# Later modulation vectors in steps of 1,024 columns, reduced by 32x32 transposes on VectorE, and the first two vectors with the ada matrix as the stationary operand

## The chip, the cores and the metric

The kernel runs on 1 core of one Trainium2 chip. The metric is device time in microseconds of that core, from its start to its end, as the median of several runs; lower is better. All arithmetic is fp32 or sums of fp32r products (each operand split into a high part and a remainder, three products kept).

## The reference, cut to what matters

Two transformer blocks run one after the other on a sequence of 512 tokens of width 1024. Each block takes six modulation vectors (shift, scale and gate, once for the mixer and once for the feed-forward part) from a small condition vector. The first block also needs the first two of them for a context of 256 tokens, from a second condition vector.

```python
def adaln(cond, w, b):
    return jnp.split(jax.nn.silu(cond) @ w + b, N_MOD, axis=-1)      # w: 1024 x 6144

# first block
sh_a, sc_a, gt_a, sh_f, sc_f, gt_f = adaln(c, w_ada[0], b_ada[0])
csh_a, csc_a, ...                  = adaln(c_ctx, w_ada[0], b_ada[0])
h_ctx = modulate(rms_norm(ctx, g_mix_pre), csh_a, csc_a)
h_lat = modulate(rms_norm(x, g_mix_pre), sh_a, sc_a)
x = x + gt_a * rms_norm(token_mixer(h_lat, ...), g_mix_post)
x = x + gt_f * rms_norm(conv_ffn(modulate(rms_norm(x, g_ffn_pre), sh_f, sc_f), ...), g_ffn_post)
# second block: the same six vectors from silu(c_2) @ ada_w_2 + ada_b_2, a hybrid mixer, a SwiGLU
```

The products of a condition vector with its matrix (w_ada, ada_w_2) are the subject here: 12 vectors of 1024 values, so 48 MB of weights that are each used once.

## The kernel before, in words

Activations lie with the features on the 128 partitions and the 512 tokens along the free dimension (8 tiles of 128x512). Weights stream from HBM in 110 chunks of 128x2048 (1 MB) through two buffers `raw`; ScalarE makes the high part WH of a chunk (`split_hi`), VectorE the remainder WL (`split_lo`), and TensorE multiplies both with the high and low parts of the activations: three fp32r matmuls for every product (`mm3`, L1158 to L1162). The order of all work is written out by hand: each engine has its own program (`@block.sync`, `.scalar`, `.vector`, `.tensor`), and counting semaphores tie them. The stages in order are: start (norm statistics and the first two modulation vectors), k and v, q, retention, Fourier mix, gate, output projection (C_OUT), the up projection with a convolution (C_UP, 22 tiles, a hardware loop `Fori` of 11 passes on every engine), the down projection (C_DOWN, 12 chunks), then the second block (C_U, C_K2, C_V2, C_Q2, C_GATES, attention, C_MERGE, C_O, C_UP2, C_DOWN2).

The modulation vectors are made in two ways.

The first two (shift and scale of the first mixer, for the tokens and for the context) are made at the start. Eight chunks `adaf` of 128x2048 (256 columns of the matrix for all 1024 rows) are loaded first of all. For each chunk TensorE holds the two condition vectors as the stationary operand (128x2, `csil`) and streams 256 columns of the matrix past them, 8 times with accumulation (L1227). The result is two rows of 256 values; ScalarE copies four pieces of 512 of them out of PSUM (L405, `m0row`), and TensorE turns them into columns with a 2x2 identity (`mod0_turn`, L1220). Between chunks TensorE also sums squares for the norms of the context (L1232) and of x (L1235). VectorE then adds the bias (L769) and the norms and the first projection follow. A matmul of fp32 operands shows in the trace as two passes, each with a weight load of its own.

The other ten vectors are made during the later stages, in 40 jobs of 256 columns (`ada_job`, L715). A job loads 128x2048 in two halves `ada_half`, and VectorE multiplies each of 8 pieces of 128x256 by one column of the condition vector and adds it to `ada_acc` (L706, L708). The remaining sum over the 128 partitions is TensorE's (`ada_sum`, L1192 to L1195): two fp32 matmuls with 128 columns of `ada_acc` as the stationary operand and a column of ones as the moving one. These calls stand between the projections in TensorE's program: after every k/v, q, f, g and out chunk, once in each pass of the up loop, after every one of the 12 down chunks and after the 4 chunks of C_U. VectorE adds the bias in `modulation` (L993) before a vector is needed.

VectorE's program puts a job behind a `split_lo` or behind the last use of a tile; in the last part of a stage the output tiles (`out_tile`, L941) come behind it.

Of the kernel before, what the change touches and what calls it, by code (L numbers as in the profile page):

```python
# [19 lines left out]
P = 128  # L20
# [30 lines left out]
ADA_LATER = 40  # L51
JOBS_UP = 14
JOBS_DOWN = JOBS_UP + FT // 2

# [25 lines left out]
def build(nc, weights, ada, x_t, ctx_t, vecs, rope, band, pos, csd, masks, out):  # L80
# [4 lines left out]
    with stack:  # L85
# [17 lines left out]
        csil_up = fix("csil_up", [P, FT // 2, KT])  # L103
        rstd = fix("rstd", [P, L])
        scratch = fix("scratch", [P, 2, L])
        ada_acc = fix("ada_acc", [P, 2, 256])
        mod0 = fix("mod0", [P, 16, 2])
        mod = fix("mod", [P, 2 * ADA_LATER])
# [4 lines left out]
        ident2 = fix("ident2", [2, 2])  # L113
# [7 lines left out]
        ada_half = fix("ada_half", [P, 2, CH // 2])  # L121
# [13 lines left out]
        m0row = over("m0row", [2, 16 * P], U + 64 * KB)  # L135
# [33 lines left out]
        spL = (over("spL0", [P, 1280], H0 + 5 * KB, R), over("spL1", [P, 1280], U + 101 * KB, R))  # L169
# [4 lines left out]
        mask_in = over("mask_in", [P, 4, P], U + 58 * KB)  # L174
        lnsq = over("lnsq", [P, CT, L], U + 96 * KB)
        cH, cL = over("cH", [P, CT, L], U, R), over("cL", [P, CT, L], U + 8 * KB, R)
        assert U + 106 * KB <= nc.sbuf_usable_end, (U, nc.sbuf_usable_end)
# [66 lines left out]
        def _(sp):  # L244
            sp.dma_start(vec[:, :], vecs).then_inc(s.vec_in, 16)
            sp.dma_start(ctxT[:, :, :], ctx_t).then_inc(s.ctx_in, 16)
            sp.dma_start(ident2[:, :], masks[0:2, 0, 0:2]).then_inc(s.ident2_in, 16)
# [9 lines left out]
            for j in range(2):  # L257
                sp.dma_start(ada_half[:, j, :], ada[ADA_FIRST, :, j * (CH // 2):(j + 1) * (CH // 2)])\
                    .then_inc(ada_in[j], 16)
# [8 lines left out]
            def load_half_job(a, j):  # L268
                sp.wait_ge(s.ada_read, 2 * a + (j - 1))
                sp.dma_start(ada_half[:, j, :], ada[a + ADA_FIRST, :, j * (CH // 2):(j + 1) * (CH // 2)])\  # L270
                    .then_inc(ada_in[j], 16)

            def load_job(a):

                for j in range(2):
                    load_half_job(a, j)

            job = 1  # L280
            for c in range(2, C_UP + 3):
                load_chunk(c, c % 2)
                if c == 2 or c - 2 in (C_DFT + 1, C_G):
                    continue
                load_job(job)
                job += 1
            assert job == JOBS_UP + 1, job
            load_chunk(C_UP + 3, 1)

            with sp.Fori(0, FT // 2) as i:  # L290
                for j in range(2):
                    load_chunk(2 * i + (C_UP + 4 + j), j)
                    load_half_job(i + JOBS_UP + 1, j)

            load_job(JOBS_DOWN + 1)
            with sp.Fori(0, 6) as i:
                for j in range(2):
                    load_chunk(2 * i + (C_DOWN + 4 + j), j)
                    load_job(2 * i + (JOBS_DOWN + 2 + j))
            load_chunk(C_DOWN + 16, 0)  # L300
            load_job(ADA_LATER - 1)
            load_chunk(C_DOWN + 17, 1)
# [32 lines left out]
        def _(act):  # L335
# [67 lines left out]
            for q in range(4):  # L403
                act.wait_ge(s.mod0_sum, 2 * q + 2)
                A(m0row[:, 4 * P * q:4 * P * (q + 1)], bank[q][0:2, :], ACT.Copy).then_inc(s.mod0_row, 1)  # L405
                if q == 2:

                    act.wait_ge(s.csd_in, 16)
                    A(csdH[:, :], csd_in[:, :], ACT.Copy).then_inc(s.csd_hi, 1)
                    split_hi(0, 0, True)  # L410
# [172 lines left out]
            with act.Fori(0, FT // 2) as i:  # L583
                for j in range(2):
                    for x, tmp in enumerate((tA, tB)):
                        act.wait_ge(s.mm_done, 32 * i + done(C_UP + j, x, 2))

                        w = VAT["cw"] + 2 * FT + x * FT + j
                        b = VAT["cb"] + x * FT + j
                        A(tmp[:, j, :], bank[2 * j + x][:, :], ACT.Identity, bias=vec[:, bass.ds(2 * i + b, 1)],  # L590
                          scale=vec[:, bass.ds(2 * i + w, 1)]).then_inc(s.conv_mid, 1)
                    split_hi(2 * i + (C_UP + j + 2), j)
                    act.wait_ge(s.bank_free, 4 * i + (B_UP + 2 * j + 1))
                    A(tA[:, j, :], tA[:, j, :], ACT.Silu).then_inc(s.ffn_silu, 1)
                    act.wait_ge(s.ffn_mul, 2 * i + j + 1)
                    A(GH[:, bass.ds(2 * i + j, 1), :], tB[:, j:j + 1, :], ACT.Copy).then_inc(s.ffn_hi, 1)
# [94 lines left out]
        def _(dve):  # L691
# [8 lines left out]
            def ada_half_job(a, slot, half, c_col):  # L700

                dve.wait_ge(ada_in[half], 16 * a + 16)
                for k in range(4):
                    w = ada_half[:, half, 256 * k:256 * k + 256]
                    if half == k == 0:
                        ins = TS(ada_acc[:, slot, :], w, c_col(0), None, mult)  # L706
                    else:
                        ins = STT(ada_acc[:, slot, :], w, c_col(4 * half + k), ada_acc[:, slot, :], mult, add)  # L708
                    if k < 3:
                        own.link(ins)  # L710
                    else:
                        ins.then_inc(s.ada_read, 1)
                        dve.wait_ge(s.ada_read, 2 * a + (half + 1))

            def ada_job(a, slot, c_col, first=False):  # L715
                if not first:
                    dve.wait_ge(s.ada_summed, a - 1)
                for half in range(2):
                    ada_half_job(a, slot, half, c_col)

            ada_next = [0]

            def ada_now():
                a = ada_next[0]
                ada_next[0] += 1
                ada_job(a, a % 2, (lambda k: csil[:, k, 0:1]) if a < 16 else (lambda k: csil2[:, k:k + 1]), a < 2)
# [31 lines left out]
            for i in range(FT // 2):  # L758
                own.link(V.tensor_copy(csil_up[:, i, :], csil[:, :, 0] if JOBS_UP + i < 16 else csil2[:, :]))
# [6 lines left out]
            dve.wait_ge(s.mod0_done, 4)  # L766
# [30 lines left out]
            for p in range(2):  # L797
# [18 lines left out]
                ada_now()  # L816
# [9 lines left out]
                ada_now()  # L826
# [8 lines left out]
            for p in range(2):  # L835
# [7 lines left out]
                if p == 0:  # L843
                    states_lo(1)
                    ada_now()
# [46 lines left out]
            ada_now()  # L892

            for p in range(2):
# [7 lines left out]
                if p == 0:  # L902
                    ada_now()
            for g in range(GROUPS + 1):
# [9 lines left out]
                if g in (1, 2):  # L914

                    a = ada_next[0]
                    if g == 1:
                        dve.wait_ge(s.ada_summed, a - 1)
                    ada_half_job(a, a % 2, g - 1, lambda k: csil[:, k, 0:1])
                    ada_next[0] += g - 1  # L920
# [30 lines left out]
            def add_and_norm(m, free0):  # L951
# [3 lines left out]
                if m == 0:  # L955
                    modulation(13, 8, 24, 2)
# [13 lines left out]
            def out_phase(m, c0, free0, jobs=0):  # L970
                post_gain(m)
                for p in range(4):
                    split_lo(c0 + p + 1, (p + 1) % 2)
                    for _ in range(jobs):
                        ada_now()
# [4 lines left out]
            def down_phase(m, c0, free0, skip):  # L980
                post_gain(m)
                for p in range(4):
                    for j in range(3):
# [3 lines left out]
                        if m == 1:  # L987
                            ada_job(a, (a + 1) % 2, lambda k: csil2[:, k:k + 1])
# [716 lines left out]
```

## Time and profile before

| | |
|---|---|
| time, median of 3 runs | 1509.86 us (1508.96 to 1511.58) |
| the profiled execution's own time | 1509.9 us |
| its span | 1508.1 us |
| granted TensorE clock, mean over the span | 0.972 |
| TensorE busy with matmuls | 1435.9 us, 95%, 6532 instructions |
| VectorE busy | 913.5 us, 61% |
| ScalarE busy | 521.4 us, 35% |
| DMA | 173.56 MB, mean 115 GB/s |

TensorE's busy time is made of instructions that overlap each other, so the useful figure is the pace: the distance from one start to the next. A clock of 1.00 in a row is the upper of two levels (2.4 GHz), 0.50 the lower (1.2 GHz). The record of the clock begins at 14.7 us; the rows before that show 1.00, and there only the pace of the matmuls tells the level. A wait in brackets at the end of a row is idle time of that engine before it and what ended it.

### The profile page before, as it was taken

To read this page: it belongs to the slowest core of one execution; us is meant where nothing else is said; L and a number is where in the kernel's file an instruction comes from. 1 tells how busy PE (TensorE), PEld (TensorE's weight loads), DVE (VectorE), ACT (ScalarE), POOL (GpSimd) and SP (SyncE) were. 2 spreads that over 40 slices of the span, in tenths; PEclk is the share of its full clock that TensorE was granted. 3 is DMA by queue.
4 is the path that set the end of the run, shared out by engine and by line. 5 is a ranking of instruction groups with operands and counts; after the bars stand their busy time and mean duration, and the time that the engine had idled before them with its cause. 6 is when DMAs were issued, how large, how long until landed. Compare 5 with 4: busy or idle time off the path is not lost.

```text
span 1508.1 us, 17436 instructions
## 1 busy us (share of the span) xinstructions
PE 1435.9 (95%) x6532; PEld 1150.3 (76%) x6532; DVE 913.5 (61%) x1263; ACT 521.4 (35%) x661; POOL 26.4 (2%) x22
## 2 busy tenths in 40 slices
PE   7899999979999999998899999999979999999995
PEld 3698588848888888886689887668848888888884
DVE  2776864877677677676669883766564333332334
ACT  4432433334343433222421223773233232323211
POOL 0000000010000000001000000000010000000001
PEclk9999999979999999999899999899989999999998
DMA  9234033613434435564232222002302322222321
GB/s 394 96 116 151 13 126 136 213 56 114 164 125 147 145 126 191 193 214 168 71 132 96 101 86 82 1 1 84 112 28 84 111 84 103 92 93 102 112 84 56
DMA packets 31018, 173.56 MB, mean 115 GB/s; under 512 B 3445, under 2 KB 3701, under 8 KB 15477
## 3 DMA queue, kind: packets, MB, share of 16 engines
q1 hardware_dynamic: 30964, 172.83, 31.9%
q8 instruction: 36, 0.59, 0.2%
q14 instruction: 18, 0.14, 0.0%
HBM read 170.72 MB, written 2.10 MB: 115 GB/s over the span
## 4 chain that ended last, share of the span: by engine, by line
PE 91%; DVE 5%; ACT 2%; issue 1%; DMA 0%; SPq 0%; DVEq 0%; ACTq 0%
PE bank L1160 27%; PE bank L1161 27%; PE bank L1162 27%; PE bank L1227 2%; PE bank L1413 2%; PE bank L1573 1%; DVE xT L959 1%; DVE tmp L734 1%; PE bank L1335 1%; DVE yT L958 1%; PE bank L1559 1%; PE bank L1195 1%; PE bank L1560 1%; PE bank L1548 0%; DVE ada_acc L708 0%
## 5 line engine op out<-in xcount | busy, mean ns | idle before, releaser
L1160 PE MATMUL bank<-hH,WH 128*128 128x512 f32 x1088 | 431.3, 396 | 16.9 <-DVE hL L739 16.9
L1161 PE MATMUL bank<-hL,WH 128*128 128x512 f32 x1088 | 426.8, 392 | 0.0
L1162 PE MATMUL bank<-hH,WL 128*128 128x512 f32 x1088 | 426.7, 392 | 0.0
L698 DVE TENSOR_TENSOR WL<-raw,WH 128x2048 fp32r<-128x2048 f32 x110 | 252.0, 2291 | 165.7 <-ACT WH L343 165.0
L343 ACT ACTIVATE WH<-raw 128x2048 fp32r<-128x2048 f32 x110 | 210.1, 1910 | 150.5 <-PE bank L1162 149.7
L1160 PEld LDWEIGHTS bank<-hH,WH 128*128 128x128 f32 x1088 | 206.7, 190 | 62.6 <-issue 20.3
L1161 PEld LDWEIGHTS bank<-hL,WH 128*128 128x128 f32 x1088 | 206.8, 190 | 43.1 <-issue 1.0
L1162 PEld LDWEIGHTS bank<-hH,WL 128*128 128x128 f32 x1088 | 206.4, 190 | 43.5
L1160 PE MATMUL bank<-GH,WH 128*128 128x512 f32 x352 | 137.9, 392 | 0.0
L1161 PE MATMUL bank<-GL,WH 128*128 128x512 f32 x352 | 136.9, 389 | 0.0
L1162 PE MATMUL bank<-GH,WL 128*128 128x512 f32 x352 | 136.9, 389 | 0.0
L708 DVE SCALAR_TENSOR_TENSOR ada_acc<-ada_half,csil,ada_acc 128x256 f32<-128x256 f32 x203 | 98.4, 485 | 7.4
L1147 DVE TENSOR_TENSOR tB<-tA,bank 128x512 f32<-128x512 f32 x22 | 15.1, 688 | 113.0 <-PE bank L1162 113.0
L1063 DVE SCALAR_TENSOR_TENSOR cacc<-uT,vec,cacc 128x511 f32<-128x511 f32 (+29 forms) x120 | 78.6, 731 | 0.0
L1162 PEld LDWEIGHTS bank<-GH,WL 128*128 128x128 f32 x352 | 66.1, 188 | 13.8
L1160 PEld LDWEIGHTS bank<-GH,WH 128*128 128x128 f32 x352 | 66.1, 188 | 13.3
L1161 PEld LDWEIGHTS bank<-GL,WH 128*128 128x128 f32 x352 | 66.1, 188 | 13.2
L944 DVE TENSOR_SCALAR yT<-bank,gp 128x512 f32<-128x512 f32 x32 | 23.9, 751 | 47.8 <-ACT scratch L541 44.5
L541 ACT ACTIVATE scratch<-bank 128x512 f32<-128x512 f32 x28 | 16.8, 600 | 101.5 <-PE bank L1162 101.3
L684 ACT ACTIVATE tA<-bank 128x512 f32<-128x512 f32 x22 | 13.2, 599 | 94.7 <-PE bank L1162 94.7
L708 DVE SCALAR_TENSOR_TENSOR ada_acc<-ada_half,csil_up,ada_acc 128x256 f32<-128x256 f32 x77 | 37.2, 484 | 9.6
L1227 PE MATMUL bank<-adaf,csil 128*2 128x256 f32 x128 | 31.2, 405 | 9.0 <-DMA adaf<-ada 9.0
(255 smaller groups left out, 1872.5 us busy)
## 6 DMA issues: line engine op xcount, KB each, us to landing
raw<-weights SPq DMA_DIRECT2D x110, 1024.0 KB, 4.7
ada_half<-ada SPq DMA_DIRECT2D x80, 512.0 KB, 3.8
adaf<-ada SPq DMA_DIRECT2D x8, 1024.0 KB, 17.6
xT<-x_t SPq DMA_DIRECT2D x2, 1024.0 KB, 11.8
out_t<-xT SPq DMA_DIRECT2D x8, 256.0 KB, 2.0
ctxT<-ctx_t SPq DMA_DIRECT2D x1, 1024.0 KB, 5.1
ropeT<-rope SPq DMA_DIRECT2D x1, 512.0 KB, 21.8
bandT<-band SPq DMA_DIRECT2D x1, 448.0 KB, 19.5
```

What stands on the lines that cost most here:

```text
L343: A(WH[:, slot, :], raw[:, slot, :], ACT.Copy).then_inc(s.hi_done, 1)
L541: A(to, bank[n % 4][:, :], ACT.Square).then_inc(s.ysq_ready, 1)
L698: TT_(WL[:, slot, :], raw[:, slot, :], WH[:, slot, :], sub).then_inc(s.lo_done, 1)
L708: ins = STT(ada_acc[:, slot, :], w, c_col(4 * half + k), ada_acc[:, slot, :], mult, add)
L944: TS(yT[:, n, :], bank[n % 4][:, :], gp[:, n:n + 1], None, mult).then_inc(s.bank_free, 1)
L1063: STT(cacc[:, k, shift:L], uT[:, k, 0:L - shift], w, cacc[:, k, shift:L], mult, add)\
L1147: TT_(tB[:, j, :], tA[:, j, :], bank[2 * j + 1][:, :], mult).then_inc(s.bank_free, 2)
L1160: mm(o, lh, rh, start=start, stop=False, skip_group_check=skip)
L1161: mm(o, lh, rl, start=False, stop=False, skip_group_check=skip)
L1162: return mm(o, ll, rh, start=False, stop=stop, skip_group_check=skip)
L1227: ins = mm(bank[c // 2][0:2, 256 * (c % 2):256 * (c % 2) + 256], csil[:, k, :], adaf[:, c, 256 * k:256 * k + 256], start=(k == 0), stop=(k ...
L1413: mm(bank[5][:, :], ones[:, :], squares[k % 4], start=(k == 0), stop=(k == KT - 1))\
```

## The change

The first two vectors: for each chunk, 128 columns of the matrix are now the stationary operand and the two condition vectors (128x2) the moving one, so the result stands in columns at once. The copies by ScalarE (`m0row`), the turns by TensorE and the small identity go.

The later vectors: a step is now one row block of 128 rows times 1,024 columns; 8 steps make one whole vector (a group), 80 steps all ten. Each step is one VectorE instruction on 128x1024. After the eighth VectorE transposes the accumulator in blocks of 32x32 (into the weight buffer) and sums along the free axis, which leaves, for each quarter of the partitions, the partial sums of 32 columns in `quarter`. TensorE adds the four quarters with a stacked identity `selT`, for one, two or four vectors at a time (`mod_sum`), in 5 places in all. The loops of the up stage of the first block are written out on all four engines. Some buffers are placed elsewhere (`lnsq`, `spL`, `mask_in`), and the loads of the steps replace those of the half jobs in the sync queue, two for one.

```diff
-                for k in range(KT):
-                    ins = mm(bank[c // 2][0:2, 256 * (c % 2):256 * (c % 2) + 256], csil[:, k, :],
-                             adaf[:, c, 256 * k:256 * k + 256], start=(k == 0), stop=(k == KT - 1))
+                for j in range(2):
+                    t = 2 * c + j
+                    for k in range(KT):
+                        at = 256 * k + P * j
+                        ins = mm(bank[4][:, 2 * t:2 * t + 2], adaf[:, c, at:at + P], csil[:, k, :], start=(k == 0),
+                                 stop=(k == KT - 1), skip_group_check=True)
                 ins.then_inc(s.mod0_sum, 1)
...
-                if c >= 3 and c % 2:
-                    mod0_turn(c // 2 - 1)
-            mod0_turn(3)
...
-            def ada_sum(a, slot, col):
-                pe.wait_ge(s.ada_read, 2 * a + 2)
-                for j in range(2):
-                    ins = mm(bank[7][:, col(j)], ada_acc[:, slot, P * j:P * j + P], ones[:, 0:1], start=True, stop=True,
-                             skip_group_check=True)
-                ins.then_inc(s.ada_summed, 1)
+            def mod_sum(first, groups):
+                pe.wait_ge(s.ada_read, KT * (first + groups))
+                for q in range(4):
+                    at = 32 * first + q
+                    ins = mm(bank[7][32 * q:32 * q + 32, KT * first:KT * (first + groups)], selT[:, :],
+                             quarter[:, at:at + 32 * groups - 3:4], start=True, stop=True, skip_group_check=True)
+                ins.then_inc(s.mod_summed, 1)
...
+            def ada_step():
+                a = ada_next[0]
+                ada_next[0] += 1
+                group, k = divmod(a, KT)
+                w = ada_half[:, a % 2, :]
+                c_col = csil[:, k, 0:1] if group < 4 else csil2[:, k:k + 1]
+                dve.wait_ge(ada_in[a % 2], 16 * (a // 2) + 16)
+                if k == 0:
+                    TS(ada_acc[:, :], w, c_col, None, mult).then_inc(s.ada_read, 1)
+                    return
...
+                ins = STT(ada_acc[:, :], w, c_col, ada_acc[:, :], mult, add)
+                if k < KT - 1:
+                    ins.then_inc(s.ada_read, 1)
+                    return
+                own.link(ins)
+                own.link(V.transpose(w, ada_acc[:, :]))
+                V.tensor_reduce(quarter[:, 32 * group:32 * group + 32], w.rearrange("p (b i) -> p b i", i=32),
+                                mybir.AxisListType.X, add).then_inc(s.ada_read, 1)
...
-            with pe.Fori(0, FT // 2) as i:
-                for j in range(2):
-                    have(2 * i + (C_UP + j))
...
+            for t in range(FT):
+                j = t % 2
+                have(C_UP + t)
```

The five calls of `mod_sum` on TensorE stand behind the gate chunks (one vector), before the norm sum of the first output projection (two), behind the up stage (two), behind the fourth down chunk (one) and behind C_Q2 (four). VectorE takes two steps where it took a job, with these exceptions: the four parts of the first output projection take 2, 1, 1 and 0 steps; each of the 22 up tiles takes one step (before: half a job); the four chunks of C_U take 3, 3, 3 and 1.

## Rows read from the trace of the kernel before

**Rows 1.** The chain that ended last, shares of the span by engine (page).
```profile
PE 91%; DVE 5%; ACT 2%; issue 1%; DMA 0%; SPq 0%; DVEq 0%; ACTq 0%
```
**Rows 2.** The waits of TensorE: waiting line, releaser, us in total, times, longest.
```profile
PE bank L1413 <- ACT scratch L387: 18.1, 6, 5.3
...
PE bank L1160 <- DVE aF L879: 3.7, 1, 3.7
```
**Rows 3.** Timeline, TensorE in the start stage: start us, us, line, count.
```profile
9.02 6.40 PE L1227 MATMUL bank<-adaf,csil 128*2 128x256 f32 x16 [9.02 <-DMA adaf<-ada]
...
15.97 7.07 PE L1227 MATMUL bank<-adaf,csil 128*2 128x256 f32 x32
22.97 1.12 PE L1235 MATMUL bank<-sqacc,ones 128*128 128x512 f32 x2
...
43.53 1.94 PE L1220 MATMUL bank<-ident,m0row 2*128 2x2 f32 x16
```
**Rows 4.** Timeline, VectorE at the end of the start stage.
```profile
45.51 0.18 DVE L769 TENSOR_TENSOR mod<-bank,vec 128x16 f32<-128x16 f32 x1 [4.83 <-PE bank L1220]
```
**Rows 5.** Timeline, TensorE in attention, lower clock, 128-column loads.
```profile
952.73 0.41 PE L1559 MATMUL bank<-spH,maskR 128*128 128x128 f32 x1
952.94 0.41 PE L1560 MATMUL bank<-spL,maskR 128*128 128x128 f32 x1
953.15 0.52 PE L1559 MATMUL bank<-spH,maskR 128*128 128x256 f32 x1
```
**Rows 6.** Line L1560, its weight loads: ns min/median/max, first and last start.
```profile
L1560 PEld LDWEIGHTS bank<-spL,maskR x80: 187/192/333, 942.5 to 1013.5; 128*128 128x128 f32 x80
```
**Rows 7.** Windows: us, busy us (count) of PE, PEld, DVE, ACT, POOL, clock, DMA.
```profile
48.00:50.00 2.00, 0.91 (x2) 0.83 (x3) 2.00 (x4) 1.40 (x3) 0.00 (x0) 0.70 0.00 0
52.00:54.00 2.00, 2.00 (x9) 1.59 (x9) 2.00 (x4) 1.11 (x2) 0.00 (x0) 0.94 0.00 0
332.00:334.00 2.00, 0.37 (x1) 0.40 (x2) 2.00 (x4) 1.58 (x3) 0.00 (x0) 0.53 0.00 0
338.00:340.00 2.00, 2.00 (x8) 1.61 (x7) 2.00 (x4) 1.24 (x2) 0.00 (x0) 0.76 0.00 0
```
**Rows 8.** Windows in attention, the same columns.
```profile
940.00:942.00 2.00, 2.00 (x10) 1.20 (x9) 0.81 (x3) 1.86 (x7) 0.00 (x0) 1.00 0.00 0
942.00:944.00 2.00, 2.00 (x12) 1.62 (x12) 1.15 (x4) 1.94 (x5) 0.00 (x0) 0.78 0.00 0
```
**Rows 9.** Line L1195, the sums over partitions.
```profile
L1195 PE MATMUL bank<-ones,ada_acc x160: 164/250/250, 87.1 to 777.2; 128*128 128x1 f32 x160
```
**Rows 10.** Timeline, TensorE around one such sum in the up stage.
```profile
347.09 0.50 PE L1195 MATMUL bank<-ones,ada_acc 128*128 128x1 f32 x4
347.45 0.48 PE L1160 MATMUL bank<-hH,WH 128*128 128x512 f32 x1
347.77 0.39 PE L1161 MATMUL bank<-hL,WH 128*128 128x512 f32 x1
348.00 0.39 PE L1162 MATMUL bank<-hH,WL 128*128 128x512 f32 x1
```
**Rows 11.** Groups of VectorE by form: count, busy us, mean ns, idle us before.
```profile
L708 DVE SCALAR_TENSOR_TENSOR ada_acc<-ada_half,csil,ada_acc 128x256 f32<-128x256 f32 x203 | 98.4, 485 | 7.4
...
L1063 DVE SCALAR_TENSOR_TENSOR cacc<-uT,vec,cacc 128x510 f32<-128x510 f32 x4 | 2.8, 747 | 0.0
```
**Rows 12.** Timeline, VectorE in the q stage.
```profile
141.92 3.61 DVE L708 SCALAR_TENSOR_TENSOR ada_acc<-ada_half,csil,ada_acc 128x256 f32<-128x256 f32 x7
...
152.87 0.69 DVE L786 TENSOR_TENSOR qtmp<-bank,ropeT 128x512 f32<-128x512 f32 x1
```
**Rows 13.** Timeline, ScalarE in the q stage.
```profile
151.08 0.59 ACT L422 ACTIVATE qtmp<-bank 64x512 f32<-64x512 f32 x1
```
**Rows 14.** Timeline, VectorE at the end of the down stage.
```profile
705.12 0.75 DVE L944 TENSOR_SCALAR yT<-bank,gp 128x512 f32<-128x512 f32 x1
```
**Rows 15.** Timeline, TensorE at the end of the down stage.
```profile
706.52 1.13 PE L1406 MATMUL bank<-sqacc,ones 128*128 128x512 f32 x2 [0.80 <-DVE sqacc L949]
```

More of the change, by code:

```diff
@@ L300, in _, with load_step @@
-            load_chunk(C_DOWN + 16, 0)
-            load_job(ADA_LATER - 1)
-            load_chunk(C_DOWN + 17, 1)
+            def load_step(a):
+                sp.wait_ge(s.ada_read, a - 1)
+                sp.dma_start(ada_half[:, a % 2, :], ada_later[a]).then_inc(ada_in[a % 2], 16)
+            for c in range(2, C_OUT):
+                load_chunk(c, c % 2)
+                if c == C_G + 1:
+                    load_step(16)
+                    load_step(17)
+                elif c not in (2, C_G):
+                    load_step(2 * c - 4)
+                    load_step(2 * c - 3)
@@ L304, in _ @@
+            for q in range(12):
+                load_step(STEPS_DOWN + 2 + 2 * q)
+                load_step(STEPS_DOWN + 3 + 2 * q)
+                load_chunk(C_DOWN + 4 + q, q % 2)
+            for i in range(4):
+                for a in range(STEPS_U + 2 + 3 * i, min(STEPS_U + 5 + 3 * i, STEPS)):
+                    load_step(a)
+                if i < 2:
+                    load_chunk(C_U + 4 + i, i % 2)
             sp.wait_ge(s.mm_done, 16 * C_U)
@@ L715, in ada_job @@
[L715 to L719, printed above, removed]
             ada_next = [0]
-            def ada_now():
+            def ada_step():
                 a = ada_next[0]
                 ada_next[0] += 1
-                ada_job(a, a % 2, (lambda k: csil[:, k, 0:1]) if a < 16 else (lambda k: csil2[:, k:k + 1]), a < 2)
+                group, k = divmod(a, KT)
[5 more added lines that the diff above has]
+                    return
+                if k == 1 and group:
+                    dve.wait_ge(s.ada_read, a)
+                elif k > 1 or group:
+                    dve.wait_ge(s.ada_read, a)
+                else:
+                    dve.wait_ge(s.ada_read, 1)
+                ins = STT(ada_acc[:, :], w, c_col, ada_acc[:, :], mult, add)
[6 more added lines that the diff above has]
+                                mybir.AxisListType.X, add).then_inc(s.ada_read, 1)
@@ L728, in norm_lo, with ada_steps @@
+            def ada_steps(n):
+                for _ in range(n):
+                    ada_step()
             def norm_lo(m, tmp, src, width, hi, lo, shift, gain, mul_s, hi_s, lo_s, root=rstd):
@@ L973, in out_phase @@
                     split_lo(c0 + p + 1, (p + 1) % 2)
-                    for _ in range(jobs):
-                        ada_now()
+                    ada_steps(steps[p])
                     out_tile(m, 2 * p)
@@ L1035, in _ @@
+            modulation(3, 24, 32)
+            modulation(3, 32, 40)
             down_phase(1, C_DOWN, B_DOWN, 0)
@@ L1083, in _ @@
                 conv_taps(11)
+                if p == 1:
+                    modulation(5, 48, 80)
                 if p == 6:
@@ L1432, in out_phase @@
                         project_pair(0, src_h, src_l, order, ready, 2)
-                    for _ in range(jobs if p < 3 else 0):
-                        ada_now()
+                if m == 0:
+                    mod_sum(1, 2)
                 out_stat(m)
-                for _ in range(jobs):
-                    ada_now()
                 if m < 3:
@@ L1508, in _ @@
                     ins.then_inc(s.mm_done, step(n, 2))
+            mod_sum(6, 4)
             for i in range(16):
```

278 lines of the change are left out of this document (105 added, 173 removed).

## The prediction

> **What bounds the kernel now.** I read the chain that ended last first: TensorE holds 91% of it, VectorE 5% [rows 1]. So an edit on VectorE counts only where TensorE waits for it, and every instruction taken from TensorE's stream counts almost anywhere. The waits say where that is not so: TensorE waits mostly at the four norms (18.1 us for ScalarE's squares), which the change leaves alone, and once for 3.7 us behind VectorE between q and retention [rows 2]. Then I read the timeline of the start, because there the change alters TensorE's own work. TensorE begins at 9.02 us, when the first chunk has landed, and from then on is never idle: the first 16 passes take 6.40 us (0.40 us each), the next 32 take 7.07 us (0.22 us each), so it starts at the lower clock and reaches the upper one around 15 us; the turns end the stage and VectorE goes on at 45.51 us [rows 3, 4]. The stage is TensorE's from 9.02 to 45.5 us.
>
> **Part 1, the start: from 128 passes to 256.** Before, 8 chunks x 8 row blocks x 2 passes = 128 passes, each with a 2-column load and 256 streamed columns. After, 8 x 2 x 8 = 128 matmuls, 256 passes, each with a 128-column load and 2 streamed columns. The 32 turns go. What counts now is the pace of a 128-column load.
>
> At the upper clock the nearest row is the last set of turns: 16 passes with 128-column loads and 2 streamed columns in 1.94 us, 0.12 us each [rows 3]. At the lower clock I have no row with so few streamed columns; the nearest are the pairs in attention with 128-column loads and 128 streamed columns, which follow each other at 0.21 us (952.73, 952.94, 953.15) [rows 5]; the load itself lasts 333 ns there and 187 to 192 ns at the upper clock [rows 6]. Bounds for a pass at the lower clock: not under 0.12 us, the pace at the upper clock, and not over 0.33 us, the load if nothing overlaps it. I take 0.213 us, since the row is of the same load.
>
> Which clock? The stage begins at the lower one. Before, a dense stream lifted it. Now two columns are streamed per pass. The row that decides for me is in attention: from 940 to 944 us TensorE is busy without a gap (10 and 12 instructions in 2 us), with a load ahead of each matmul, and yet the clock falls inside the second window (mean 0.78) [rows 8]. These are matmuls of 64 rows with 128 to 512 columns, far more streaming than two columns. So loads one behind the other do not hold the clock up, and I expect them not to lift it: the whole stage runs at 1.2 GHz.
>
> The sum: 256 x 0.213 = 54.5 us. The two norm sums between the chunks run at the lower clock too: two passes of 256 columns at 0.40 us = 0.8 us, and the 512-column one twice its 1.06 us (22.97 to the next start) = 2.1 us [rows 3]. The end is 9.02 + 54.5 + 2.9 = 66.4 us, VectorE goes on at 66.6 instead of 45.5: **+21.1 us**. Nothing hides it: the norm and the first projection need these vectors. The removed copies of ScalarE and the 11 small copies of VectorE lay beside TensorE's work: 0.
>
> After the stage TensorE idles some 3.5 us and starts the first projection at the lower clock in both kernels. Before, that lasted from 49.1 to about 52.2 us (means 0.70 and 0.94); at another restart from about 333.6 to 338.9 us (0.53 and 0.76) [rows 7]. Half of such a stretch is lost, so the difference lies between -1 and +1.5 us: **+0.5**.
>
> The Trainium skill says otherwise on the load. Its page "TensorE: Matmul & The Clock Gate", section "LDWEIGHTS (loading the stationary operand)", prices a load at its columns over 1.2 GHz, so 107 ns at either clock. The trace disagrees: 192 against 333 ns [rows 6]. By the page an estimate of the 256 passes is 27 us and the start would end before 40 us.
>
> **Part 2, the sums on TensorE.** Before, 160 passes at L1195 [rows 9], 40 calls of 4. Around one: start 347.09, next projection matmul 347.45, the one after 347.77, then the usual 0.23 [rows 10]. So 0.36 us for the four, and the first matmul behind them takes 0.32 instead of 0.23: 0.45 us a call. Of the 40, five lie where TensorE waits anyway: two in the q stage ahead of the 3.7 us wait [rows 2], one ahead of the wait for the gate's silu, one behind the norm sum of the first output projection, and the last of the down stage (part 4). 35 x 0.45 = **-15.75 us**.
>
> Added are 5 calls of 4 matmuls, 8 passes, with 32-column loads and 8 to 32 columns streamed. No row has them; at the pace of L1195 (0.09 us each, and 0.09 behind them) a call costs 0.8 us, as an upper bound; the lower is 0.2 us. I take 0.8. The first stands ahead of the silu wait and is hidden; four count, also the one ahead of L1406, where TensorE came straight from the projection: **+3.2 us**.
>
> **Part 3, VectorE.** A multiply-add of 256 columns takes 485 ns, one of 510 columns 747 ns [rows 11]: 1.03 ns a column, so 1,024 columns cost 0.485 + 768 x 0.00103 = 1.28 us. A job was 8 instructions, 4.0 us; two steps are 2.6 us. Ten times come a transpose and a reduction of 1,024 columns, not in the trace: between half and twice the pace of the multiply-add, so 0.5 to 2.1 us each; I take 1.1. In the last step of a group VectorE then has 2.2 us more, so 4.8 instead of 4.0 us for a pair: hidden, because in the long stages a projection pair lasts 10.9 us (48 x 0.227 us) and VectorE needs 7 to 10 us of it. Without that cover each would cost up to 4.2 us. The later `modulation` calls wait for sums that TensorE has passed already; the one for the last 32 columns moves behind 11 convolution taps and nothing waits for it. In sync's queue every load of a step stands behind a wait that is met before the chunk load that follows it; only a third step in C_U finds its data late by some 2 us, within the slack of 10.9.
>
> In the q stage VectorE is what TensorE waits for: the seven multiply-adds from 141.92 last 3.61 us, then WL, and the last rope tile starts at 152.87 [rows 12]. Two steps are 1.4 us shorter; ScalarE's swap for that tile ends at 151.67 [rows 13], 1.2 us earlier, and moves up with the 0.45 us of the removed sum, so it is no bound: **-1.4 us**.
>
> **Part 4, the end of the down stage.** VectorE reaches the last two output tiles at 705.12 [rows 14], behind a job; TensorE has been done with its projection since 705.2 and starts L1406 at 706.52, after a wait of 0.80 us [rows 15]. With two steps VectorE is 1.4 us earlier, L1406 starts at 705.3, and the last square of ScalarE is ready when it ends: **-1.2 us**, the removed sum included.
>
> **Loops written out.** Inside the loop the pace is 0.23 us as elsewhere, no gap at a turn: 0. Written-out stages elsewhere run at the same pace, so fetching more code costs nothing I can see; bounds -0.2 and +2 us.
>
> **The sum** against the profiled span: 1508.1 + 21.1 + 0.5 - 15.75 + 3.2 - 1.4 - 1.2 = 1514.6 us. The execution's own time is 1.8 us above its span (1509.9) and within 0.1 us of the median, so **1516.3 us**: slower by 0.4%, because 15 us gained in later stages are overpaid by 21.6 us at the start.
>
> **Rivals.** *The clock rises during the start (faster).* If loads with two streamed columns count as work, or if their pace does not hang on the clock, the passes run at 0.12 us after the first 6.4 us (30 passes): 9.02 + 6.4 + 226 x 0.12 + 1.6 = 44.1 us, 1.4 us earlier than before instead of 21.1 later, and no other term changes: 1516.3 - 22.5 = 1493.8 us. For it: before, the clock rose within 7 us of steady work [rows 3]. Against: it fell in attention under unbroken pairs [rows 8]. It decides where the stage ends before about 57 us (1516.3 - 9.5 = 1506.8); a rise at 30 us would do, with 95 passes before it and 161 behind: an end near 50 us and 1500 us in all. The same page of the Trainium skill, in "What's actually happening", says that activity releases the throttle and speaks of whatever is issued, which by itself would be this rival; the trace bears the first half out, the second not. Chance 0.11.
>
> *Nothing overlaps the load.* 256 x 0.333 = 85 us, 30.7 more: 1547 us. For it only the 333 ns; against it, 0.21 us between two such loads [rows 5]. Chance 0.04.
>
> *VectorE comes late.* Transposes at 2.1 us and late third steps push it over the 10.9 us of a pair in the up stage or C_U; three or four stalls of 1 to 2 us: 1521 us. Chance 0.05.
>
> **How the numbers follow.** The forecast has 0.80; its own range is 1509 to 1524 us (pace 0.20 to 0.24 us: -3 and +7; sums 5 us cheaper to 1 dearer). That range with the third rival holds 0.8, so the range is 1508 to 1524. What a measurement of this kernel can tell from no change is about 0.2%, 1506.8 to 1512.9 us. Faster 0.14 (first rival, and a tail of the forecast), same 0.09, slower 0.77.
>
> **What would show it.** Right: L1227's successor with 256 passes at about 0.21 us, VectorE's first mod0 addition near 66.6 us, 40 passes of `mod_sum` in place of 160, no gap of TensorE behind the last down chunk, and from the first projection on about 15 us less than before. Wrong: a pace near 0.12 us in the start or a clock record that begins there at 1.00; a new wait of TensorE for VectorE in the up stage or the convolution; a gain in the later stages under 10 us, which would mean that the 0.45 us are not saved.

## The result and the profile after

The changed kernel takes **1518.85 us** (median of 4 runs, 1518.31 to 1521.63), the one before on the same chip 1509.49 us (4 runs, 1508.96 to 1511.58): ratio 1.0063, 95% interval 1.0046 to 1.0081. 1516.3 us had been forecast. The profiled execution took 1518.31 us, its span is 1516.4 us, 8.3 us more than before.

The page of the changed kernel: span, busy time by engine, shares of the chain that ended last, and three groups (count, busy us, mean ns, idle us before).
```profile
span 1516.4 us, 16108 instructions
...
PE 1444.9 (95%) x6508; PEld 1176.0 (78%) x6508; DVE 880.0 (58%) x1033; ACT 516.2 (34%) x657; POOL 26.4 (2%) x22
...
PE 90%; DVE 6%; ACT 2%; issue 1%; DMA 1%; SPq 0%; DVEq 0%; ACTq 0%
...
L1196 PE MATMUL bank<-csil,adaf 128*128 128x2 f32 x256 | 54.7, 352 | 8.9 <-DMA adaf<-ada 8.9
L1196 PEld LDWEIGHTS bank<-csil,adaf 128*128 128x128 f32 x256 | 55.2, 333 | 10.1 <-issue 9.9
L713 DVE SCALAR_TENSOR_TENSOR ada_acc<-ada_half,csil,ada_acc 128x1024 f32<-128x1024 f32 x70 | 89.7, 1281 | 11.4 <-DMA ada_half<-ada_later 9.1
```
The chain has the same shape as before [rows 1]: TensorE still sets the time, so the 8.3 us must be in its own stream. L1196 has 256 loads with a mean of 333 ns, the figure that the loads of the lower clock have in [rows 6]. That is the first term of the prediction in one row.

The start stage of the changed kernel, TensorE's timeline; it answers to [rows 3].
```profile
8.93 6.96 PE L1196 MATMUL bank<-csil,adaf 128*128 128x2 f32 x32 [8.93 <-DMA adaf<-ada]
15.75 1.20 PE L1201 MATMUL bank<-csqacc,ones 128*128 128x256 f32 x2
16.74 13.65 PE L1196 MATMUL bank<-csil,adaf 128*128 128x2 f32 x64
30.25 2.05 PE L1204 MATMUL bank<-sqacc,ones 128*128 128x512 f32 x2
32.10 34.13 PE L1196 MATMUL bank<-csil,adaf 128*128 128x2 f32 x160
69.86 0.77 PE L1148 MATMUL bank<-hH,WH 128*128 128x512 f32 x1 [3.62 <-DVE hL L738]
```
The same stage on VectorE; it answers to [rows 4].
```profile
66.27 0.17 DVE L766 TENSOR_TENSOR mod<-bank,vec 128x16 f32<-128x16 f32 x1 [27.22 <-PE bank L1196]
```
160 passes in 34.13 us are 0.213 us each, from the first to the last. VectorE goes on at 66.27 us, where 66.6 was forecast.

Windows of the changed kernel in this stage: us, busy us (count) of PE, PEld, DVE, ACT, POOL, granted clock, DMA share, GB/s.
```profile
20.00:66.00 46.00, 46.00 (x211) 44.97 (x211) 5.82 (x10) 7.78 (x19) 0.00 (x0) 1.00 0.52 215
```
Here is a trap. The clock column says 1.00 while the loads last 333 ns. It says 1.00 at the start of the kernel before too, where 16 passes of 256 columns take 6.40 us [rows 3]. The column has no record until the clock changes for the first time, and nothing changed it here: the record of the changed kernel begins at 73.5 us, where the 512-column matmuls of the first projection go from 0.43 us to 0.23 us each. The duration of a known load is the safer reading: 192 ns at 2.4 GHz, 333 ns at 1.2 GHz.

Next I followed the distance between the same matmul in both traces (after minus before). It is +20.8 us at the first projection, +22.3 in the k/v stage, +16.2 ahead of the first norm behind it (309 us in the kernel before), +6.7 just before attention, +10.2 behind it, and +8.3 at the end. Two of the steps up were not in the sum. In the k/v stage TensorE waits for `ktmp` in both kernels, 2.29 us before and 2.09 us after, but only in the changed one does the clock fall behind the wait. The first row is of the kernel before, the other two of the changed one:
```profile
70.00:72.00 2.00, 2.00 (x19) 2.00 (x19) 1.07 (x2) 1.48 (x3) 0.00 (x0) 1.00 0.91 385
90.00:92.00 2.00, 1.46 (x7) 1.49 (x8) 1.09 (x2) 1.53 (x3) 0.00 (x0) 0.64 0.88 365
92.00:94.00 2.00, 2.00 (x11) 2.00 (x11) 1.58 (x3) 0.28 (x1) 0.00 (x0) 0.50 0.27 111
```
And in attention the clock falls in both kernels, for longer in the changed one. The kernel before in windows of 7 us:
```profile
943.00:950.00 7.00, 4.62 (x18) 3.65 (x17) 5.34 (x11) 4.85 (x13) 0.00 (x0) 0.51 0.00 0
950.00:957.00 7.00, 7.00 (x22) 5.11 (x21) 3.99 (x11) 5.00 (x12) 0.00 (x0) 0.52 0.02 5
957.00:964.00 7.00, 7.00 (x36) 4.78 (x37) 5.24 (x12) 4.95 (x14) 0.00 (x0) 1.00 0.00 0
```
The changed kernel, the same stage:
```profile
951.00:957.00 6.00, 3.22 (x11) 2.66 (x11) 5.12 (x10) 3.87 (x12) 0.00 (x0) 0.50 0.00 0
957.00:964.00 7.00, 7.00 (x22) 5.07 (x21) 3.79 (x11) 4.90 (x11) 0.00 (x0) 0.50 0.00 0
964.00:971.00 7.00, 7.00 (x18) 3.94 (x17) 3.40 (x8) 2.55 (x8) 0.00 (x0) 0.50 0.00 0
```
The lower clock lasts 13.7 us before (943.1 to 956.8) and 20.5 us after (950.7 to 971.2), and the distance grows by 3.45 us there. The change touches nothing in that stage but the place of the buffer `spL`. Whether it caused this was one question for the experiments.

### The profile page after: what moved, and what is told of

Same layout as the page of the kernel before. It is cut to its first block, busy times and chain, and to the rows that moved or that the text cites. A ratio compares the mean times of both kernels' runs of the same rounds, so it can differ in the third digit from the quotient of the medians.

```text
span 1516.4 us, 16108 instructions
## 1 busy us (share of the span) xinstructions
PE 1444.9 (95%) x6508; PEld 1176.0 (78%) x6508; DVE 880.0 (58%) x1033; ACT 516.2 (34%) x657; POOL 26.4 (2%) x22
## 4 chain that ended last, share of the span: by engine, by line
PE 90%; DVE 6%; ACT 2%; issue 1%; DMA 1%; SPq 0%; DVEq 0%; ACTq 0%
PE bank L1148 27%; PE bank L1150 26%; PE bank L1149 26%; PE bank L1196 4%; PE bank L1376 2%; PE bank L1528 1%; DVE xT L951 1%; DVE tmp L733 1%; PE bank L1298 1%; DVE yT L950 1%; PE bank L1514 1%; PE bank L1515 1%; DVE ada_acc L713 1%; PE bank L1503 0%; DMA adaf<-ada 0%
## 5 line engine op out<-in xcount | busy, mean ns | idle before, releaser
L713 DVE SCALAR_TENSOR_TENSOR ada_acc<-ada_half,csil,ada_acc 128x1024 f32<-128x1024 f32 x70 | 89.7, 1281 | 11.4 <-DMA ada_half<-ada_later 9.1
L1150 PEld LDWEIGHTS bank<-GH,WL 128*128 128x128 f32 x352 | 66.1, 188 | 13.7
L1196 PE MATMUL bank<-csil,adaf 128*128 128x2 f32 x256 | 54.7, 352 | 8.9 <-DMA adaf<-ada 8.9
L1196 PEld LDWEIGHTS bank<-csil,adaf 128*128 128x128 f32 x256 | 55.2, 333 | 10.1 <-issue 9.9
L1009 DVE SCALAR_TENSOR_TENSOR tB<-bank,vec,tB 128x504 f32<-128x504 f32 x22 | 16.3, 743 | 68.6 <-ACT tB L584 68.5
```

What stands on the lines that cost most here:

```text
L713: ins = STT(ada_acc[:, :], w, c_col, ada_acc[:, :], mult, add)
L1009: own.link(STT(to[:, :, 1:ROW], b[:, :, 0:ROW - 1], v("cw", w), to[:, :, 1:ROW], mult, add))
L1150: return mm(o, ll, rh, start=False, stop=stop, skip_group_check=skip)
L1196: ins = mm(bank[4][:, 2 * t:2 * t + 2], adaf[:, c, at:at + P], csil[:, k, :], start=(k == 0), stop=(k == KT - 1), skip_group_check=True)
```

## The experiments

My theory: the start costs 21 us because a pass is priced by its load, and the load's pace by the clock, which two streamed columns do not lift; the 40 small sums gave back 0.45 us each. The rivals: the pace has another cause (the chunks' DMA, the load itself), or the later part costs something that the start hides. Each kernel is compared with the kernel before on its own chip; the median of that one was 1510.4 to 1510.8 us.

**One part undone, and one part alone.** `e1_old_start` is the changed kernel with the start of before, `e2_new_start_alone` the kernel before with the new start.
```diff
 # e1_old_start, against after
-    for j in range(2):
-        t = 2 * c + j
-        for k in range(KT):
-            at = 256 * k + P * j
-            ins = mm(bank[4][:, 2 * t:2 * t + 2], adaf[:, c, at:at + P], csil[:, k, :], ...)
+    for k in range(KT):
+        ins = mm(bank[c // 2][0:2, 256 * (c % 2):256 * (c % 2) + 256], csil[:, k, :],
+                 adaf[:, c, 256 * k:256 * k + 256], ...)
+    if c >= 3 and c % 2:
+        mod0_turn(c // 2 - 1)
...
```


> The changed kernel with only its start undone: the condition vectors are stationary again, the ada chunk streams, and the copies and turns are back; the later steps, mod_sum and the written-out loops stay. Theory (slow weight loads at the lower clock cost about 21 us in the start, the rest of the change gains about 13 us net in this execution's clock phases): 1518.9 - 20.9 = 1498 us, between 1493 and 1502, first mod0 addition of VectorE back at 45.5 us. Rival (the later part gains nothing or costs by itself, and the start costs little): 1509 us or more.

> The kernel before with only the new start (ada chunk stationary, two columns streamed). Theory: 1509.5 + 21 = 1530.5 us, 256 passes at 0.213 us, first mod0 addition near 66 us. Rival (the start's cost comes from something that the later part brings with it, such as moved buffers): 1510 to 1516 us.

`e1_old_start`: 1497.94 us (6 runs, 1492.62 to 1500.74), ratio 0.9919 [0.9903, 0.9934]. `e2_new_start_alone`: 1530.55 us (4 runs), ratio 1.0137 [1.0123, 1.0152]; VectorE goes on at 66.29 us; the distance to before is +20.8 us at the first projection, +22.1 in the k/v stage and +20.9 at the end. +20.15 and -12.46 us add up to +7.7, where the medians of both parts together differ by +9.4 and their spans by +8.3. That fits within the spread of `e1_old_start`, 8 us from its fastest run to its slowest, so nothing shows that one part changes the other. The later part alone is a gain.

**Is it the clock?** `e3_warm_new_start` puts 22 matmuls of `ones` with itself ahead of the first chunk, `e4_warm_old_start` does the same to `e1_old_start`. Their results are not used.
```diff
+for _ in range(22):
+    mm(bank[7][:, 0:P], ones[:, :], ones[:, :], start=True, stop=True, skip_group_check=True)
```


> The changed kernel with 22 matmuls of ones by ones (128 columns) on TensorE before the first chunk lands, so that the clock is at its upper level when the narrow passes begin. Theory (narrow passes neither lift nor hold the clock): the first passes run at 0.11 to 0.12 us, then the clock falls and the rest at 0.213; 3 to 7 us at the upper level save as much again, 1512 to 1516 us. Rival (narrow passes can't lift the clock but hold it): all 256 at 0.12 us, 1518.9 - 22 = 1497 us. Second rival (the load pace does not hang on the clock): no change at all, 1519 us.

> e1_old_start with the same 22 matmuls of ones ahead. Theory: the first chunk's 16 passes take 3.5 instead of 6.4 us, the stage ends 2 to 3 us earlier, 1495 to 1496 us if e1 is 1498. Rival (the stage waits for the chunks' landing then): no gain over e1.

`e3_warm_new_start`: 1517.35 us (4 runs), ratio 1.0044 [1.003, 1.0059]. TensorE's timeline:
```profile
1.03 7.27 PE L1189 MATMUL bank<-ones 128*128 128x128 f32 x44 [1.03 <-POOL ones L323]
...
8.75 3.75 PE L1198 MATMUL bank<-csil,adaf 128*128 128x2 f32 x32 [0.45 <-DMA adaf<-ada]
...
13.35 13.65 PE L1198 MATMUL bank<-csil,adaf 128*128 128x2 f32 x64
```
Its windows:
```profile
8.00:12.00 4.00, 3.55 (x33) 3.39 (x31) 2.12 (x5) 1.60 (x4) 0.00 (x0) 1.00 1.02 430
12.00:14.00 2.00, 2.00 (x11) 1.82 (x10) 0.00 (x0) 0.00 (x0) 0.00 (x0) 0.57 0.99 418
14.00:20.00 6.00, 6.00 (x29) 6.00 (x30) 1.28 (x2) 2.30 (x4) 0.00 (x0) 0.50 1.02 426
```
The loads of the first chunk in this run:
```profile
L1198 PEld LDWEIGHTS bank<-csil,adaf 128*128 128x128 f32 x30 | 3.4, 192 | 0.6 <-issue 0.6
```
At the upper clock the same instruction runs at 0.113 us (32 passes start to start in 3.61 us), with the DMA as busy as elsewhere in the stage, so the pace is the clock's doing. But the narrow passes do not hold it: it falls at 12.27 us and the other 224 passes run at 0.213 again. VectorE goes on at 62.88 us, 3.4 us earlier. In the profiled execution 3.3 us of that are lost in attention: the lower clock lasts 30.7 us there, the distance to before grows by 6.8 us instead of 3.45, and the span is 1516.5 us against 1516.4.

These rows also say what makes the new start dear. An estimate from them and [rows 3]: at the upper clock the old form would cost 128 x 0.221 = 28.3 us and the new one 256 x 0.113 = 28.9 us; at the lower clock 128 x 0.40 = 51.2 and 256 x 0.213 = 54.5 us. At the same clock the two forms are nearly equal. The difference of 21 us is mostly that the stream of the old form was followed by a rise of the clock 5.7 us after it began, and the stream of the new one ran for 57 us without one.

The Trainium skill's "TensorE: Matmul & The Clock Gate", section "LDWEIGHTS (loading the stationary operand)", gives a load as its columns over 1.2 GHz, 107 ns for 128 columns, with no word on the gated clock. The pace of 113 ns at the upper clock is near that figure, the 213 ns at the lower clock is twice it; here the measurement decides.

`e4_warm_old_start` missed what I wrote: 1499.35 us (5 runs, 1497.67 to 1500.35), no better than without the 22 matmuls. Its timeline says why:
```profile
9.04 3.61 PE L1214 MATMUL bank<-adaf,csil 128*2 128x256 f32 x16 [1.15 <-DMA adaf<-ada]
...
18.76 3.62 PE L1214 MATMUL bank<-adaf,csil 128*2 128x256 f32 x16 [1.93 <-DMA adaf<-ada]
...
23.00 1.13 PE L1222 MATMUL bank<-sqacc,ones 128*128 128x512 f32 x2 [0.63 <-DVE sqacc L759]
```
The first 16 passes need 3.61 instead of 6.40 us, and then TensorE waits 1.93 us for the third chunk and 0.63 us for the squares, and is back at its old time, 23.00 against 22.97 [rows 3]. Up to there the old start has to wait for its data once TensorE is faster; the new one is paced by its loads. From 23 us on TensorE is busy without a gap in the old form too.

**Can denser work between the narrow passes hold the clock?** `e8_dense_every_second` puts one such dense matmul behind every second narrow matmul but the last of a block, `e9_dense_every_one` behind every one but the last, both on top of the 22.
```diff
 for k in range(KT):
     ins = mm(bank[4][:, 2 * t:2 * t + 2], adaf[:, c, at:at + P], csil[:, k, :], ...)
+    if k % 2 == 1 and k < KT - 1:      # e9: k % 1 == 0
+        mm(bank[7][:, 0:P], ones[:, :], ones[:, :], start=True, stop=True, skip_group_check=True)
```


> e3_warm_new_start plus one dense matmul (ones by ones, 128 columns, two passes, result unused) behind every second narrow matmul of the start, 48 in all. If this much dense work holds the clock: 256 x 0.113 + 96 x 0.107 = 39 us, the stage ends near 50 us, 16 us less than the changed kernel. If not (dense passes are then a quarter of the time): the clock falls as in e3 and the added passes cost 96 x 0.21 = 20 us, end near 83 us. I expect the second.

> The same with a dense matmul behind seven of eight narrow ones, 112 in all. If the clock holds: 256 x 0.113 + 224 x 0.107 = 53 us, end near 64 us. If not: 54.5 + 47.7 = 102 us, end near 112 us. I expect the first: a narrow pass is slow only for the clock, and at the upper level its pace is 0.113 us throughout.

`e8_dense_every_second`: 1540.59 us in one run, the clock falls at 10.72 us, VectorE goes on at 85.13. `e9_dense_every_one`: 1564.94 us in one run, it falls at 11.17, VectorE goes on at 112.0. The windows of `e9_dense_every_one`:
```profile
9.00:12.00 3.00, 3.00 (x24) 3.00 (x25) 1.33 (x4) 0.83 (x2) 0.00 (x0) 0.86 1.01 429
12.00:15.00 3.00, 3.00 (x16) 3.00 (x16) 0.00 (x0) 0.00 (x0) 0.00 (x0) 0.50 0.99 421
```
I had expected that a nearly even mix would hold the clock; it did not, though a stream of such dense matmuls alone had lifted it just before. So filling of this kind does not repair the start. The 96 passes of `e8_dense_every_second` cost 85.13 - 62.88 = 22.3 us, 0.23 us each, which is 0.21 at the lower clock and a part from the earlier fall of the clock, by 1.6 us. Wider filling, of 512 columns, was not tried here.

**The lower clock in attention.** `e1_again` is `e1_old_start` run a second time. `e5_attention_fill` adds three unused matmuls of 512 columns in each of the first five turns of attention to `e1_old_start`; `e10_before_attention_fill` adds the same to the kernel before.
```diff
+if 0 <= i <= 4:
+    for _ in range(3):
+        mm(bank[4][:, :], maskR[:, 3, :], maskR[:, :, :], start=True, stop=True, skip_group_check=True)
```


> e1_old_start once more on the same chip as e5 and e6, for its spread: median 1498 us, runs from 1492 to 1501 by the length of the lower-clock stretch in attention.

> e1_old_start plus 15 matmuls of 512 columns on masks (three in each of TensorE's first five turns of the attention loop, results unused), where TensorE waits and the clock falls. Theory A (the spread of 1491 to 1499 us of e1, and part of what the changed kernel lost against the sum, is the stretch at the lower clock in attention, 13.7, 20.5 or 30.7 us long, 0.5 us lost per us): the clock stays up, e1's profiled span less 8 to 10 us plus 2 us for the added work, 1489 to 1492 us median and a spread under 3 us. Rival B (the attention stage is slower for moved buffers): no gain, 1498 to 1500 us.

> The kernel before with the 15 filling matmuls in attention alone. Theory (the stretch at the lower clock in attention was there before too, 13.7 us in its profile, 7 us lost): the time falls by 7 - 2 = 5 us, 1505.5 us, with no lower clock in attention. Rival (only the changed later part loses its clock there): no gain, or 2 us more.

`e1_again`: 1497.56 us (4 runs, 1495.18 to 1500.3). The same kernel, profiled twice, has a span of 1491.5 and of 1498.5 us. In the second the lower clock in attention lasts from 926.1 to 956.9 us, 30.7 instead of 20.5. There is one stretch more, 3.4 us behind the wait for `ktmp` at 69.4 us, the one at 154.7 us lasts 6.8 instead of 3.4 us, and two at the norms 10.2 instead of 6.8 us. The stretch behind `ktmp` costs 1.35 us here, with the old start: that step, too, belongs to the execution and not to the new start. Its windows in attention:
```profile
934.00:941.00 7.00, 7.00 (x23) 5.57 (x22) 5.18 (x13) 4.13 (x10) 0.00 (x0) 0.50 0.00 0
948.00:955.00 7.00, 7.00 (x22) 5.16 (x22) 3.89 (x8) 2.51 (x5) 0.00 (x0) 0.50 0.00 0
955.00:962.00 7.00, 7.00 (x31) 4.64 (x30) 3.32 (x8) 4.08 (x11) 0.00 (x0) 0.87 0.01 2
```
Those of `e5_attention_fill`:
```profile
927.00:934.00 7.00, 6.87 (x36) 4.85 (x36) 5.35 (x11) 4.85 (x13) 0.00 (x0) 1.00 0.00 0
941.00:948.00 7.00, 7.00 (x37) 5.08 (x37) 4.92 (x12) 5.11 (x13) 0.00 (x0) 1.00 0.00 1
```
36 (six of them filling) and 37 passes in 7 us instead of 22 and 23. `e5_attention_fill` takes **1488.32 us** (4 runs, 1486.09 to 1490.59), ratio 0.9851 [0.9836, 0.9866], 9.2 us less than `e1_again` on the same chip, for 15 more matmuls. `e10_before_attention_fill` takes 1506.85 us (10 runs), ratio 0.9977 [0.9968, 0.9987], 3.6 us less than before (5 us had been expected), where the stretch that it removes was 13.7 us long. With the stretch filled in both, the later part is worth more: -22.5 us with it against -3.6 without, so 18.9 us instead of 12.5 to 13.3.

Over all profiles without filling in attention the stretch lasted 13.7 us (before, `e2_new_start_alone`), 20.5 (after, `e1_old_start`) or 30.7 (`e3_warm_new_start`, `e4_warm_old_start`, `e7_no_transpose`, `e8_dense_every_second`, `e9_dense_every_one`, `e1_again`). It differs between two profiles of one kernel, so one profile of a kernel is no measure of it. But the eight with the new later part all have 20.5 or 30.7, the two without it 13.7, and the 37 runs of the kernel before lie within 3.2 us while the 10 of `e1_old_start` and `e1_again` spread over 8.1. That the later part makes the stretch longer is therefore likely; what would do it was not tested.

**Do the transposes and reductions cost anything?** `e7_no_transpose` is `e1_old_start` with two copies of 32 columns in their place; its later modulation vectors are not the sums.
```diff
-own.link(V.transpose(w, ada_acc[:, :]))
-V.tensor_reduce(quarter[:, 32 * group:32 * group + 32], w.rearrange("p (b i) -> p b i", i=32),
-                mybir.AxisListType.X, add).then_inc(s.ada_read, 1)
+own.link(V.tensor_copy(quarter[:, 32 * group:32 * group + 32], ada_acc[:, 0:32]))
+V.tensor_copy(w[:, 0:32], quarter[:, 32 * group:32 * group + 32]).then_inc(s.ada_read, 1)
```


> e1_old_start without the ten transposes and reductions of 1,024 columns on VectorE; two copies of 32 columns stand in their place, so the later modulation vectors are not the sums. Theory: they are hidden, same as e1, 1491 to 1500 us, and TensorE's distances up to the second norm unchanged. Rival (they delay a split or a tile): 2 to 5 us faster in the up or q stage.

1498.71 us in one run. Just before attention it is 16.5 us ahead of before; `e1_old_start` is 17.9, `e1_again` 14.8 and `e5_attention_fill` 16.0 us ahead. VectorE is busy 20.5 us less (859.6 against 880.1 us), and no gain outside that spread shows: the transposes and reductions are hidden, as far as a spread of 3 us can tell.

**All restarts filled.** `e6_all_fill` adds matmuls of `ones` to `e5_attention_fill` wherever TensorE waits for a norm.
```diff
+for _ in range(15):                      # behind the start, before the first projection
+    mm(bank[7][:, 0:P], ones[:, :], ones[:, :], start=True, stop=True, skip_group_check=True)
...
+fill(32)                                 # the same matmul, ahead of the sums of squares of a norm
...
+    fill(2 if k < KT - 1 else 15)        # behind each of them
```


> e5 plus dense matmuls of ones by ones (unused results) where TensorE idles: 15 before the first projection, 32 ahead of each sum of squares of x, 2 between its parts and 15 behind it. Theory: the projections behind each norm and behind the start begin at the upper clock, 2.5 us each for four of them, and the squares' sums are not paced by the clock: 8 to 10 us under e5, 1480 to 1483 us. Rival (the fill delays the sums of squares by as much): no gain over e5.

**1487.31 us** (5 runs, 1486.82 to 1488.25), ratio 0.9846 [0.9833, 0.986]: the lowest median here, but only 1 us under `e5_attention_fill`, which the intervals do not tell apart, and not the 8 to 10 us that I had written. The page's row of the clock in 40 slices (mean 0.993) has nearly all of it at the upper level; two stretches of 3.4 and 6.8 us are left, at 69.1 and 154.4 us. The projection behind the first filled norm starts at full pace:
```profile
PEclk9999999999999999999999999999999999999998
```
```profile
326.22 3.51 PE L1396 MATMUL bank<-ones 128*128 128x128 f32 x30
330.79 0.47 PE L1156 MATMUL bank<-hH,WH 128*128 128x512 f32 x1 [1.06 <-DVE hL L746]
331.10 0.39 PE L1157 MATMUL bank<-hL,WH 128*128 128x512 f32 x1
```
The rival I had named took a good part of the gain back: the unused passes stand ahead of and between the sums of squares, which end 0.6, 0.7 and 1.4 us later at the three filled norms, counted from the last projection ahead of them, than in `e5_attention_fill`. What it does buy is a small spread, 1.4 us over 5 runs.

## Why the prediction was right

**The start, +21.1 forecast.** Right in mechanism and size: +20.8 us at the first projection in the changed kernel, +20.9 with the start alone. The assumed pace of 0.213 us was the measured one. One of the listed signs against the forecast was a clock record that begins there at 1.00. The column stands at 1.00 in the stage, but the record begins only at 73.5 us, behind it; read from the column, that sign means nothing, since before shows 1.00 there too. The first rival, that the clock rises in this stage, is out: it would have needed 0.12 us passes, which come only behind other matmuls and last 3.5 us (`e3_warm_new_start`). The second (nothing overlaps the load) is out by the pace.

**The restart behind the start, +0.5 forecast.** Within 0.3 us of nothing: the distance at the start of the first projection and behind it hardly differs. What the sum lacked is the next restart, behind `ktmp`, +1.5 us.

**The sums, -15.75 and +3.2 forecast.** The gain is right: between 345 and 566 us of the kernel before the distance falls by 4.54 us over ten calls. The price of the new sums was too high. The one behind the up stage of the first block in the changed kernel:
```profile
592.84 0.39 PE L1150 MATMUL bank<-hH,WL 128*128 128x512 f32 x1
593.16 0.26 PE L1183 MATMUL bank<-quarter,selT 128*32 128x16 f32 x8
593.35 0.50 PE L1148 MATMUL bank<-GH,WH 128*128 128x512 f32 x1
593.69 0.39 PE L1149 MATMUL bank<-GL,WH 128*128 128x512 f32 x1
593.92 0.40 PE L1150 MATMUL bank<-GH,WL 128*128 128x512 f32 x1
```
From 592.84 to 593.69 are 0.85 us where two ordinary steps are 0.46: about 0.4 us for eight passes, half of the 0.8 that I took; the distance puts 0.38 to 0.48 us on the calls ahead of the norm, behind the up stage and behind C_Q2. This term was mis-sized by some 1.6 us in four calls. The loads of these passes are of 32 columns and last 106 to 110 ns, those of L1195 of 128 columns and 187 to 192 ns; whether that is the reason was not tested.

**VectorE.** The multiply-add was forecast at 1.28 us and is 1.281. The three new forms by group:
```profile
L719 DVE STREAM_TRANSPOSE ada_half<-ada_acc 128x1024 f32<-128x1024 f32 x10 | 12.5, 1245 | 0.3
L720 DVE TENSOR_REDUCE quarter<-ada_half 128x32 f32<-128x1024 f32 x10 | 12.2, 1220 | 0.3
L705 DVE TENSOR_SCALAR ada_acc<-ada_half,csil 128x1024 f32<-128x1024 f32 x10 | 7.5, 746 | 0.0
```
1.245 and 1.22 us against 1.1 taken. VectorE idles 9.1 us for `ada_half`, 5.6 of them at two late steps in C_U, yet TensorE's waits hold nothing new of weight:
```profile
PE bank L1376 <- ACT scratch L389: 18.4, 6, 5.7
...
PE bank L1148 <- DVE aF L876: 3.0, 1, 3.0
...
PE bank L1148 <- DVE WL L692: 0.2, 1, 0.2
```
The q stage's wait is 3.0 instead of 3.7 us [rows 2], and from 120 us to behind the wait the distance falls by 2.1 us, where one sum (0.45) and the 1.4 were forecast. Part of the earlier end of VectorE stays a wait, because TensorE reaches it earlier by its two removed sums. The third rival, VectorE late, is out by the 0.2 us here and by `e7_no_transpose`.

**The end of the down stage, -1.2 forecast.** Nearly as put, -1.07 us: the norm sum had come 1.3 us behind TensorE's last projection [rows 15]; now no sum stands between them and the gap is 0.23 us.
```profile
713.35 0.39 PE L1150 MATMUL bank<-GH,WL 128*128 128x512 f32 x1
713.81 1.12 PE L1369 MATMUL bank<-sqacc,ones 128*128 128x512 f32 x2
```
**What was missing: the clock's stretches.** From the first projection to just before attention the later part was to give -15.15 us; the changed kernel gave -14.0, `e1_old_start` -17.9, `e1_again` -14.8, `e5_attention_fill` -16.0. In the changed kernel the cheaper sums (-1.6) were offset by the restart behind `ktmp` (+1.5) and by the first norm (+0.95 behind its new sum; its cause stays open). Then attention cost +3.45 us, and the third norm gave back 1.9. With 0.8 us less than forecast at the start and its restart, that makes the +8.3 us of span where 6.5 were forecast. So the mechanism is right and the closeness of the total is in part luck: terms of 1 to 3.5 us that were not in the sum, or too high in it, stood against each other. The step that was put at nothing is the stretch in attention [rows 8], taken as common to both kernels. It is common, but its length is not fixed. What decides between 13.7, 20.5 and 30.7 us stays open: it shifts without an edit, and the later part may make it longer, which was not tested.

## What to carry to other kernels

With few columns to stream, a matmul is paced by its load (0.113 us here, 0.213 at the lower clock). At the same clock that made the two forms of this product nearly equal; what counted was that the wide stream was followed by the upper clock and the narrow one was not. So in a stage that starts at the lower clock, keep the narrow vector stationary and stream the wide matrix. Small sums between long matmuls are worth collecting, 0.45 us a call for four passes here, as VectorE had room for the transposes. Before a stage where the clock is seen to fall under unbroken work, try a few unused wide matmuls: 15 of them gave 9.2 us with the new later part and 3.6 us without it, and less spread is a result too.

## What the hardware showed that was not expected

- A load of 128 columns lasts 192 or 333 ns and follows the next at 0.113 or 0.213 us, by the clock alone (`e3_warm_new_start`). The Trainium skill's "TensorE: Matmul & The Clock Gate" says in "What's actually happening" that activity releases the throttle. Here the trace agrees only in part: the clock rose behind the streams of dense matmuls, but in the changed kernel TensorE was busy for 46.00 of 46 us and it was not released. Which instructions are issued matters, not only that some are.
- A mix did not hold the clock either: with 112 dense matmuls among 128 narrow ones it fell at 11.17 us (`e9_dense_every_one`).
- The clock column stands at 1.00 until its first change, also where the loads show 1.2 GHz.
- One kernel's profiled spans differ by 7.0 us (1491.5 and 1498.5), with longer and more stretches of the lower clock in the second; 3.4 us of it arise in attention. In such a kernel a term under 3 us can only be read from the distance between the same instructions in two traces, not from the span.
